# Hybrid pooling / gated-linear-attention trunk on eight cores: two kinds of transposes moved from TensorE to DMA transposes, first loads reordered, pool groups reordered

## What is computed

```
h = concat(meta, x)                                   # (2064, 1024) per core
for i in range(4):
    a = rmsnorm(h, norm_i)                            # y * rsqrt(mean(y*y)+eps) * gain
    if i is even:                                     # pool layer
        u, z = split(a @ w_in)                        # 2048 channels each, 4 groups of 512
        for group g, window w in (2, 4, 8, 16):
            t = trailing_mean(u_g, w) - u_g
            y_g = (t @ w_grp[g]) * scale_g * silu(z_g)
        h = h + y @ w_out
    else:                                             # GLA layer, 4 heads, dk 256, dv 512
        q, k, v, z, low = split(a @ w_in)
        cum = chunk_cumsum(logsigmoid(low @ w_gate2 + b) / 16)
        qe, ke = q * exp(cum) / 16, k * exp(-cum)
        o  = mask(qe ke^T) v + qe S                   # S: carried state, 256 x 512
        S  = exp(cum_end) * (S + ke^T v)
        h = h + (rmsnorm_head(o) * silu(z)) @ w_out
out = rmsnorm(h, final_norm)[16:]
```

## Time and profile before

| | us |
|---|---|
| three timed runs, median (range) | 2213.58 (2203.5 to 2215.14) |
| the profiled execution: its time | 2216.9 |
| its span, first to last instruction, core 7 (slowest) | 2214.9 |
| spans of the eight cores | 2195.1 to 2214.9 |
| busy in the span: PE / DVE / ACT / POOL | 1978.5 / 1327.1 / 1365.1 / 428.5 |
| share of the chain that ended last: PE / DVE / ACT / POOL / DMA | 79% / 6% / 4% / 3% / 2% |

### The profile page before, as it was taken

One profiled execution on the slowest core, in us unless ns is written; L12 is line 12 of the kernel. 1 busy time (PEld: TensorE's weight loads), 2 busy tenths in 40 slices (PEclk: granted clock), 3 DMA queues, 4 the chain that ended last, 5 costly groups with the idle time before them and its releaser, 6 DMA issues.

```text
span 2214.9 us, 46775 instructions; the slowest of 8 cores (2195.1 to 2214.9 us)
## 1 busy us (share of the span) xinstructions
PE 1978.5 (89%) x16712; PEld 1406.1 (63%) x16712; DVE 1327.1 (60%) x2151; ACT 1365.1 (62%) x2903; POOL 428.5 (19%) x468
## 2 busy tenths in 40 slices
PE   0289999987999999996775999999989999999997
PEld 0267777765766777664443666777656676777764
DVE  1245555775776666664443445557857766666787
ACT  2455555576676677675544545555766666676776
POOL 1012345673000000000000113447730000000000
PEclk9899999999999999998876789999999999999998
DMA  9313132303013040020201131423030040400011
GB/s 187 96 30 58 18 61 39 59 10 61 1 23 57 2 78 2 2 49 1 39 3 27 29 47 21 68 39 58 1 67 2 9 70 2 78 2 1 21 68 67
DMA packets 16691, 86.07 MB, mean 39 GB/s; under 512 B 2624, under 2 KB 3536, under 8 KB 9296
## 3 DMA queue, kind: packets, MB, share of 16 engines
q0 software_dynamic: 10560, 63.53, 17.0%
q1 hardware_dynamic: 5904, 19.57, 2.6%
HBM read 138.22 MB, written 8.39 MB: 66 GB/s over the span
## 4 chain that ended last, share of the span: by engine, by line
PE 79%; DVE 6%; issue 5%; ACT 4%; POOL 3%; DMA 2%; SPq 0%; DVEq 0%; ACTq 0%; POOLq 0%
PE ps L401 77%; DVE hnb L432 2%; DMA h<-x 2%; PE ps L409 2%; POOL SB L437 2%; ACT hnb L426 1%; DVE h L432 1%; POOL SA L437 1%; DVE Y L437 1%; ACT gs L426 1%; ACT rstd L426 1%; ACT hnT L426 1%; DVE S L432 0%; DVE SB L432 0%; DVE sz L432 0%
## 5 line engine op out<-in xcount | busy, mean ns | idle before, releaser
L401 PE MATMUL ps<-hnT,W 128*128 128x256 bf16 (+1 forms) x9216 | 988.0, 265 | 12.9 <-ACT vb L426 5.9
L401 PEld LDWEIGHTS ps<-hnT,W 128*128 128x128 bf16 x9216 | 834.8, 99 | 148.5 <-issue 26.8
L401 PE MATMUL ps<-W,Y 128*128 128x512 bf16 x1024 | 249.8, 386 | 15.8 <-DVE Y L437 9.3
L401 PE MATMUL ps<-W,hnT 128*128 128x512 bf16 x1088 | 261.6, 385 | 0.6 <-DVE sz L432 0.6
L437 DVE TENSOR_TENSOR h<-h,ps 128x512 f32<-128x512 f32 x256 | 175.0, 684 | 129.7 <-PE ps L401 127.6
L401 PE MATMUL ps<-W,yT 128*128 128x512 bf16 x1024 | 250.0, 387 | 0.3 <-DVE S L432 0.3
L432 DVE SCALAR_TENSOR_TENSOR h<-ps,rs,h 128x512 f32<-128x512 f32 x256 | 191.0, 746 | 98.5 <-ACT rs L426 56.8
L442 POOL COPY el<-Eq 128x2 f32<-128x2 f32 x136 | 26.4, 194 | 988.3 <-ACT Eq L426 760.6
L426 ACT ACTIVATE Sb<-S,el 128x512 bf16<-128x512 f32 x256 | 183.3, 716 | 47.0 <-DVE S L432 29.9
L432 DVE SCALAR_TENSOR_TENSOR S<-S,el,ps 128x512 f32<-128x512 f32 x240 | 176.9, 737 | 58.7 <-PE ps L401 57.4
L432 DVE SCALAR_TENSOR_TENSOR sz<-ps,vec,gs 128x256 bf16<-128x256 f32 (+2 forms) x288 | 129.9, 451 | 118.3 <-ACT rs L426 60.6
(11 more groups left out here) (87 smaller groups left out, 2456.0 us busy)
## 6 DMA issues: line engine op xcount, KB each, us to landing
W<-wpack POOLq DMA_DIRECT2D x56, 1024.0 KB, 9.8
h<-x SPq DMA_DIRECT2D x16, 512.0 KB, 44.8
out<-h SPq DMA_DIRECT2D x16, 512.0 KB, 2.7
W<-wpack POOLq DMA_DIRECT2D x8, 512.0 KB, 6.3
gbc<-gains SPq DMA_DIRECT2D x5, 512.0 KB, 3.9
Wglr<-wglrp POOLq DMA_DIRECT2D x2, 132.0 KB, 26.0
wg<-wg2p POOLq DMA_DIRECT2D x8, 33.0 KB, 2.2
hm<-metaT SPq DMA_DIRECT2D x1, 64.0 KB, 12.6
```

Source lines behind the costliest of these rows:

```text
L401: ins = e.matmul(o_, lhsT=l_, rhs=r_, start=st, stop=sp_)
```

## The change

1. The transposes of `hnb` into `hnT` (64 tiles of 128x1024) and of `ke` into `kd` (128 tiles of 128x256) leave TensorE and the ACT copies behind them go too. Both become DMA transposes from SBUF to SBUF, all issued on SP's queue (helper `xbar`). `hnb` has two buffers now. The `kd` transpose is issued in `proj`, right behind `ke`; the masking of the meta chunk moves from `kd` to `vb`. `ke` is laid out by tile.
2. First loads: the `x` tiles go from SP's queue to ACT's, three at once, the rest each behind an earlier tile's landing; the weights of unit 0 come in the order of their use, with the fold's operand in two halves; the identity matrix goes. In the first unit the norm runs two blocks ahead, and `upart` comes before `zpart`.
3. The pool groups run in the order window 8, 16, 4, 2 (`GROUPS`).
4. The planner gives the bulk loads, `x` and the transposes a DMA channel each, with the same assumed rate. `la` and `Eq` share a buffer.

```diff
+GROUPS = (2, 3, 1, 0)
-        dma_free = 0.0
+        dma_free = {"bulk": 0.0, "x": 0.0, "tr": 0.0}
...
-    def tr(reads, writes, lst, idn):
...
-        P.op("pe", fn, reads, writes, 57.0 * len(lst), 170.0)
+    def xbar(sem, out_, in_, reads, writes, nbytes):
+        P.dma("sp", sem, lambda q: q.dma_start_transpose(out=out_, in_=in_), reads, writes, nbytes, chan="tr")
...
-    def norm_tile(i, b):
-        rms(i)
-        stt([hb[i], b_stat[i], b_gbc], [b_hnb[0]], hnb[0][:, :], h[:, i - 1, :], rstd[:, i:i + 1], gbc[:, :], ALU.mult, ALU.mult)
-        pT = PS[b][:, :].bitcast(BF16).rearrange("p (kc n) -> p kc n", kc=8)
-        tr([b_hnb[0], b_const], [bank[b]], [(pT[:, kc, :], hnb[0][:, kc * 128:(kc + 1) * 128]) for kc in range(8)], ident[:, :])
+    def norm_tile(i):
+        k = nrot[0] % 2
+        nrot[0] += 1
+        rms(i, k)
+        stt([hb[i], b_stat[i], b_gbc], [b_hnb[k]], hnb[k][:, :], h[:, i - 1, :], rstd[:, i:i + 1], gbc[:, :], ALU.mult, ALU.mult)
         c0 = tile_col0(i)
-        act([bank[b]], [hnTb[i]], hnT[:, :, c0:c0 + 128], pT, AF.Copy, psum=True)
+        xbar("hnt%d" % k, hnT[:, :, c0:c0 + 128], hnb[k][:, :], [b_hnb[k]], [hnTb[i]], 262144)
...
+                    for k, (t_, o, m) in enumerate(offs_of(bi)):
+                        if t_ < NT - 1:
+                            kn = "kd%d" % (t_ % 2)
+                            xbar(kn, T[kn][:, :].rearrange("p (f m) -> p f m", f=2), ke[:, k, :, :].rearrange("p f m -> p (f m)"),
+                                 [b_ke], [A[kn]], 65536)
...
-            if t_ < NT - 1:
-                pk = PS[4][:, 0:128].bitcast(BF16)
-                tr([b_ke, b_const], [bank[4]], [(pk[:, dc * 128:(dc + 1) * 128], ke[:, dc, o:o + 128]) for dc in range(2)], ident[:, :])
-                if t_ == 0:
-                    act([bank[4], b_m16], [A[kdn]], kd[:, :], pk, AF.Copy, scale=m16, psum=True)
-                else:
-                    act([bank[4]], [A[kdn]], kd[:, :], pk, AF.Copy, psum=True)
...
+        o = [dma("pool", "Wg", Wt[1][2][:, 2048:4096], wpack[0][:, 0:2048], [], [Wb[1][2]], 128 * 8192)]
...
+        for k in range(2):
+            o.append(dma("pool", "Wu%d" % k, dst[:, :, k * 512:(k + 1) * 512], src[:, :, k * 512:(k + 1) * 512], [], [b_wuh[k]], 1 << 20))
+        o.append(wload(0, 1, 4096, 8192, W[1][:], "W01"))
+        o.append(wload(0, 2, 8192, 12288, W[2][:], "W02"))
...
-    for i in range(1, NT):
-        dma("sp", "x%d" % i, h[:, i - 1, :], xv[:, i - 1, :], [], [hb[i]], 524288)
-    load_unit(0)
-    load_unit(1)
+    def xload(i, after=()):
+        return dma("act", "x%d" % i, h[:, i - 1, :], xv[:, i - 1, :], [], [hb[i]], 524288, chan="x", after=after)
+
+    xs = [xload(i) for i in (1, 2, 3)]
+    W0 = load_first()
+    xs += [xload(i, [W0[1]]) for i in (4, 5)]
+    for i in range(6, NT):
+        xs.append(xload(i, [xs[i - 3]]))
```

More of the change, by code:

```diff
@@ L37 @@
 class Op:
-    __slots__ = ("i", "eng", "fn", "deps", "dur", "tail", "sem", "bytes", "idx", "semval", "done", "prio", "users", "nd", "vc", "start", "tag")
+    __slots__ = ("i", "eng", "fn", "deps", "dur", "tail", "sem", "bytes", "idx", "semval", "done", "prio", "users", "nd", "vc", "start", "tag", "chan")
 class Prog:
@@ L98, in op, with dma @@
         return self._new(eng, fn, reads, writes, dur, tail)
-    def dma(self, queue, sem, fn, reads, writes, nbytes):
+    def dma(self, queue, sem, fn, reads, writes, nbytes, chan="bulk", after=()):
         op = self._new(queue, fn, reads, writes, 1000.0 if queue == "pool" else 60.0, 0.0)
-        op.sem, op.bytes = sem, nbytes
+        op.sem, op.bytes, op.chan = sem, nbytes, chan
+        for o in after:
+            op.deps.setdefault(o.i, True)
         self.dsems.setdefault(sem, 0)
@@ L332, in build @@
     gbc = sb("gbc", [128, D], F32)
-    hnb = [sb("hnb0", [128, D], BF16)]
+    hnb = [sb("hnb%d" % k, [128, D], BF16) for k in range(2)]
     PS = [E(nc.psum_tensor("ps%d" % i, [128, 512], F32)) for i in range(8)]
@@ L443, in copy, with dma @@
              dve_dur(n) if eng == "dve" else n * 1.0 + 100.0, 100.0)
[L445 to L450, removed]
+    def dma(queue, sem, out_, in_, reads, writes, nbytes, **kw):
+        return P.dma(queue, sem, lambda q: q.dma_start(out=out_, in_=in_), reads, writes, nbytes, **kw)
     b_tri = Buf("tri")
-    dma("pool", "cst2", tri[:], cst[:, 128:256], [], [b_tri], 65536)
     b_iw = b_m16 = Buf("iw")
@@ L463, in build @@
     hnorm = lambda j, c: vec[:, 32 + 16 * j + c:32 + 16 * j + c + 1]
-    units = [(li, u) for li in range(n_layers) for u in range(4)]
+    units = [(li, u) for li in range(n_layers) for u in (GROUPS if li % 2 == 0 else range(4))]
     def wload(ui, p, c0, c1, dst, name, part=None):
@@ L688, in outp @@
                             after_tile(li, t_)
-                zpart()
-                if ui == 0 and bi == 0:
-                    fold(0)
-                upart()
+                if ui == 0:
+                    if bi == 0:
+                        fold(0)
+                    upart()
+                    if bi == 0:
+                        dma("pool", "cst2", tri[:], cst[:, 128:256], [], [b_tri], 65536, after=[xs[9]])
+                        load_unit(1)
+                    zpart()
+                else:
+                    zpart()
+                    upart()
                 window()
@@ L929, in prep_inputs @@
             if li % 2 == 0:
+                u = GROUPS[u]
                 win = pool_w_in[j]
```

84 lines of the change are left out of this document (46 added, 38 removed).

## The result

| | us |
|---|---|
| changed kernel, median of four runs (range) | 2107.87 (2083.43 to 2201.33) |
| kernel before, beside it | 2213.97 (2203.5 to 2215.14) |
| ratio | 0.9494, 95% interval 0.9407 to 0.9581 |
| profiled execution of the changed kernel: time, span (core 2, the slowest) | 2109.36, 2107.8 |
| spans of its eight cores | 2047.6 to 2107.8 |

The ratio leaves out disturbed runs, the 2201.33 among them. The forecast was 1940 us, with 1890 to 2070 as its range. One thing is new that no median shows: the cores lie 60 us apart, where they lay 20 us apart before, and the metric takes the slowest.

The account below looks back on a forecast made before the run. TensorE bounds the kernel except in three kinds of stage, where it idles. Terms -60 - 70 - 129 - 6.5 - 9 = -274.5 from 2216.9 give 1942, less 3 for the median 1940 us; range 1890 to 2070.

Parts of the forecast that it names:

- the price of a transpose beside a weight load: Any 256 KB `hnb` transpose while weights stream: 7 us, against 5 us taken for an undisturbed one.
- two other rules: One DMA costs 2.0 us plus bytes at 436 GB/s; DMAs from different engines share the same 16, saving only issue time.
- rival A: All transposes take about 10 us: pool-to-head part -10 instead of -70, start loses some 20, 2020 us; chance 0.15.
- Start: Kernel start to second fold's first eviction: at 111 us instead of 171, -60 us, between -45 and -78.
- Rival B: The start gives nothing, since queues share engines and ACT's waits for `x` hold the evictions: 2000 us; chance 0.10.
- Last pool unit and first head, twice: Last fold to second head, both layer pairs: 276 us plus 13 of waits, against 330.0 and 318.1; -70 us together.
- 13 us per layer: Waits for transposes at the last pool unit's gate input: 1 us for each of five blocks, 2 for each of four.
- The length without holes: Last fold to second head: 90.3 + 36.2 + 8.5 + 139 less 2, plus 4 for handover, 276 us.
- Pool units: Pool units before the last: no term for the new group order; a unit with a fold counted at 90.3 us.
- Last head of layer 1 to the second fold of layer 2: Layer boundary no longer chained through PE's list: 195 us against 323.9, -129 us.
- the misread mark: Layer 2's second fold taken to begin at 1283.84, which is its fifth eviction; this gave the 323.9 us.
- `kd`: Later heads: 128 transpose pairs leave PE, 15 us less the three other heads' share, wait covered by projections; -9 us.

Follow-up runs that it names:

- e8: Changed kernel plus head weight loads held behind `kd` transposes, early unit loads held behind start transposes, last pool unit's gate input one block later: 0.9063 of before, 1996.02 us.
- e9: Changed kernel with the first layer's sixteen `hnT` transposes back on TensorE, copied out by ACT: 0.9494 of the kernel before.
- e3: Changed kernel with the pool groups in the old order, windows 2, 4, 8, 16: 0.9475 of the kernel before.
- thin loads: Changed kernel, each weight load from the third unit on bringing only its first 128 columns, so part of the result is wrong: 0.9089 of the kernel before.
- e4: Changed kernel with the `kd` transposes back on TensorE, copied out by ACT, `hnT` staying on DMA: 0.939 of the kernel before.

## Why the prediction was wrong

**The step that failed** is the price of a transpose beside a weight load: "At 61 KB per us a transpose would need 4.3 us and some 2.5 of fixed time: 7 us there." It took the bytes of the earlier trace rows as the share. The same row's other column, 167 packets to 166, was the rule. The `x` tiles got half the weights' bytes only because their packets are half as large; the transposes' are a thirtieth. The 2.5 us of fixed time in that sum stand in no row: alone, a whole transpose took 3.1 us. In place of 7 us the slowest core shows 32.9 and 31.1 us for the first two `hnT`, 15.7 and 12.3 at 480 us, and up to 15.1 for `kd`: each lasts until the weight queue is nearly empty. Of the 168 us, 113 go when transposes and loads are kept apart (slowest cores: 2107.8 us and, in e8, 1994.5). What is left above the forecast there is mainly the start (13) and the pool units (16 in each layer). The Trainium skill (DMA: Bandwidth & Descriptors, Queues, rings and completion order) says that each DMA engine goes round the queues packet by packet; the 226 to 224, 102 to 101 and, with small packets, 476 to 475 agree. The prediction had cited the Trainium skill for two other rules and not used this one, by which the stages beside loads cost what rival A gives or more. The Trainium skill (Advanced Engine Details and Errata, X-Bar Transpose (TRN2)) calls such transposes as fast as plain DMAs. The 3.1 us alone come near that (512 KB of gbc took 3.9 in the earlier trace rows); beside weight loads it does not hold: 0.06 MB in 10 us, where the plain loads of `x` got 0.61.

**Start (-60 forecast, -35 in the median, -24 on core 2).** Some 18 or more of the missing 25 are the transposes beside loads (e9). The rest may be the pace of `x` and the low clock, for which I had put 2 us; that is read from the views of e9 and not tested. That ACT's list decides was named; I had let it wait for `x`, and it waited for the transposes, by the squares that stand ahead of the evictions. Rival B had the wrong reason and about half the effect.

**Last pool unit and first head, twice (-70 forecast; +6 on core 2, -15 in the median).** Together 658.9 us became 664.5 and 643.4. The stalls beside loads, for which I had 13 us per layer, are worth 29 in each: with the loads held the medians are 289.8 and 296.0. These lie near the forecast's 290.9 and 291.0, but the forecast holds 13 us of stalls. The length without holes, 276 us to the `kd` mark and 278 to the `S` mark, was some 10 too short. Core 0 of e8 spent the stage without a wait for a DMA, at full clock, and PE was busy for 287.44 us. The trace of before could have told: PE was busy for 309.62 us of the same stage, so that only 22 were holes (first before, core 7, then e8, core 0; columns as above):

```profile
351.72:683.58 331.86, 309.62 (x2713) 223.16 (x2712) 226.88 (x338) 215.07 (x466) 121.53 (x99) 0.99 0.22 41
```
```profile
321.12:610.79 289.67, 287.44 (x2503) 208.42 (x2502) 206.43 (x332) 193.44 (x429) 48.98 (x64) 1.00 0.29 52
```

So two errors stand here, stalls too small and work too short, and that the first stage agrees once the loads are held is luck. The 2.6 us that the prediction worked out by the Trainium skill (DMA: Bandwidth & Descriptors, Anatomy of one DMA) come from a fit that is given there for DMAs issued by GpSimd. A transpose of SP took 3.1 us alone, a little more.

**Pool units.** The term was nought: I counted that the last unit has one POOL step instead of four, not that the second unit now has four and stretches. That cost 14 us in each pool layer by e3, whose time (0.9475) also shows that the order of groups gains nothing in sum.

**Last head of layer 1 to the second fold of layer 2 (-129 forecast, -121 measured).** The mechanism was right: the 47.7 us of waits for `hnb` are gone, and the low clock with them. The -129 rests on the misread mark; from 1275.38 the same lengths give -120. That this meets the -121 so closely is in part luck: the measured 192.4 us hold some 8 us that go with thin loads (184.7), and the forecast had none there. The times given for slices 18 to 22 (950 to 1225 us) are a slice too early as well; nothing in the sum hangs on that.

**`kd` (-9 forecast).** The cover of 4 x 1.75 us was enough for an undisturbed 2.3 us, and the size about right then: with thin loads the later heads win 6 us in all against before, and 9 against e4. Beside loads it fails, and the sign turns.

**The metric.** The prediction spoke of one core. Where a transpose meets a load is a matter of a few us and differs from core to core, so the slowest of eight pays more than the median: 2107.8 against 2071 us here, while with the loads apart all lie within 11 us. That is some 37 of the 168, and of the 113.

## What to carry to other kernels

Price a DMA that is on the critical path by its number of packets, and by the packets of what else is in flight, not by bytes: a transposing DMA with 256-byte packets is quick alone and starves beside bulk loads with large ones. Before moving work from TensorE to a DMA transpose, look where the weight loads are issued, and issue each behind the transposes that it would meet; here that was worth nearly as much as the change itself (88 to 95 us), with no byte less. And look at the spread of the cores: a wait that hits at random is paid at its worst.

## What was not expected of the hardware

The equal turns hold over an eightfold change of packet size, and for three queues at once: on core 0 between 70 and 74 us, with `x` in flight too, the packets were 58, 60 and 60. One stretch does not fit: on core 2, from 66 to 75 us, with two transposes, `x` and weight loads in flight, the packets were 148, 24 and 58, and all queues together moved 48 GB/s, against 174 between 30 and 40. A transpose issued at 60.56 us took the 35.5 us of the summary there, and a plain load of `x` 30.8. The weight loads landed at 95 us, on cores 3 and 4 at 87 and 93, and on cores 0, 5 and 7 by 78 to 83; cores 2, 3 and 4 have the latest second fold, 142 to 147 us. What slowed them was not found. The granted clock fell to 0.50, the lower of the two levels (1.2 GHz), in stretches in which PE had idled, such as 40 to 50 and 80 to 100 us on core 2, and was 1.00 again between 105 and 110 us, with PE full from 100 us on.
